# Decoder trunk: the causal mask as a matmul on TensorE, with small moves in the order of work around it

## The chip, the cores and the metric

The kernel runs on one core of one Trainium2 chip. The metric is the device time of one execution in microseconds (us); lower is better. All computing engines have their own queue of instructions and meet by semaphores: TensorE (PE in the profile, its weight loads PEld), VectorE (DVE), ScalarE (ACT), GpSimd (POOL) and SyncE (SP), whose queue issues most of the transfers.

## The reference

Two layers over 512 tokens of width 1024. The first is multi-head latent attention and a dense SwiGLU; the second a pooling mixer and a mixture of eight experts, of which each token takes two. What matters here is the attention's score block and the rows handed to the experts:

```python
for i in range(S // Q_BLOCK):                       # Q_BLOCK = 128
    q0, q1 = i * Q_BLOCK, (i + 1) * Q_BLOCK
    s = (jnp.einsum('bqhd,bkhd->bhqk', q_nope[:, q0:q1], k_nope[:, :q1])
         + jnp.einsum('bqhr,bkr->bhqk', q_rope[:, q0:q1], k_rope[:, :q1]))
    mask = jnp.arange(q0, q1)[:, None] >= jnp.arange(q1)[None, :]
    s = jnp.where(mask, s.astype(jnp.float32), -jnp.inf)
    p = jax.nn.softmax(s, axis=-1).astype(v.dtype)
    outs.append(jnp.einsum('bhqk,bkhd->bqhd', p, v[:, :q1]))
...
xb = xf[buf_tok].reshape(n_blocks, MOE_BLOCK, D)    # rows sorted by expert
yb = lax.map(expert_block, (xb, block_e)).reshape(P, D)
```

## The kernel before

Almost every product is made in three float32r matmuls (`mm3`, L1229 to L1231): each operand is split into a rounded part ("hi", made by ScalarE) and a remainder ("lo", made by VectorE), and lo x hi, hi x lo and hi x hi are summed in PSUM. So each unit of weights, 128 x 1024, is loaded by SyncE's queue, cast by ScalarE (`split`, L823) and subtracted by VectorE (`split`, L1850) before TensorE may use it. Every engine has its order of work written out by hand, and a list on one engine must match the lists on the others.

**Start.** GpSimd makes the identity `ident` (L652, L653), and TensorE fills the time until the first rows of x are there with matmuls nobody reads (`keep_clock`, L1289). Then come the normalised rows, turned by eight transposes (`norm_T`, L1241), and the down projection in four blocks of 128 tokens.

**Latents and rope.** For each block VectorE scales the latents and turns the shared rope key (`latents`), makes the remainders of the turned latents (`latents_lo`, L1909 to L1912), and turns the rope part of the queries (`rotate_q`: three products, then the add at L1888). Some of the remainders stand between the products and the add (`between`). `rope_turned` counts the turned blocks; TensorE starts the first query head when three are there.

**Attention.** Eight heads in four pairs. For each head TensorE makes scores for four blocks of queries, with 128, 256, 384 and 512 keys: one `mm3`, and two matmuls for the rope part (L1391, L1392), each block in a PSUM bank of its own. It then does filler work (projections of the next pair, or in the last pair the first parts of the output projection), turns the probabilities (ten transposes, L1402), does more filler, and multiplies by the values (L1411). Meanwhile VectorE adds the mask `causal` to the last 128 columns of each block in PSUM (L2024), takes the largest of each row (L2025), and after ScalarE's exponential (L942) divides (L2032, L2034). The order is largest 0, largest 1, divide 0, largest 2, divide 1, largest 3, divide 2, divide 3. The fourth block of scores waits for VectorE's remainder of the head before (`o_lo`, L2052). Weight splits lie at four places of each pair (`between`): after the first head's softmax, after the second's, before the second head's output, and at the pair's end.

**Dense SwiGLU.** Its first tiles (`first_tiles`) are done half by half of the tokens, because the last block's rows are turned inside them (`norm_T(2 * T - 1, ...)`).

**Experts.** GpSimd writes the rows to the experts' buffer by eight indirect DMAs (L737), each after the one before has landed, and then loads the block of the second job (L742). TensorE forms the first job's block by itself, and turns the loaded block (L1643) when it comes to the second job.

## Time and profile before

| | us |
|---|---|
| median of 3 runs | 1027.97 |
| lowest and highest | 1027.94, 1028.47 |
| the profiled execution | 1027.94 |
| its span, first to last instruction | 1026.40 |
| TensorE busy in the span | 1013.0 |
| VectorE busy | 597.0 |
| ScalarE busy | 451.4 |
| GpSimd busy | 70.5 |

The profile is of one execution, which took 1027.94 us. Busy time counts an engine's instructions, not its waits for semaphores. TensorE's ends are modelled, so in its timeline the distance from one start to the next is the thing to read, not the duration of one. The granted clock was 0.998 over the span.

### The profile page before, as it was taken

To read this page: it belongs to the slowest core of one execution; us is meant where nothing else is said; L and a number is where in the kernel's file an instruction comes from. 1 tells how busy PE (TensorE), PEld (TensorE's weight loads), DVE (VectorE), ACT (ScalarE), POOL (GpSimd) and SP (SyncE) were. 2 spreads that over 40 slices of the span, in tenths; PEclk is the share of its full clock that TensorE was granted. 3 is DMA by queue.
4 is the path that set the end of the run, shared out by engine and by line. 5 is a ranking of instruction groups with operands and counts; after the bars stand their busy time and mean duration, and the time that the engine had idled before them with its cause. 6 is when DMAs were issued, how large, how long until landed. Compare 5 with 4: busy or idle time off the path is not lost.

```text
span 1026.4 us, 15233 instructions
## 1 busy us (share of the span) xinstructions
PE 1013.0 (99%) x5570; PEld 871.8 (85%) x5570; DVE 597.0 (58%) x840; ACT 451.4 (44%) x602; POOL 70.5 (7%) x135
## 2 busy tenths in 40 slices
PE   9999999999999999999999999999999999999997
PEld 8878887798888888888888999999987888888883
DVE  6677777254344444343436760100689889898987
ACT  6445555244142322222124510010667777777764
POOL 2200000000000001010000011000000000000051
PEclk9999999999999999999999999999999999999999
DMA  9021422535463627273614749896999999999996
GB/s 293 2 82 44 137 67 74 152 104 164 138 188 95 203 85 219 93 214 94 207 41 152 269 157 336 266 343 190 336 369 386 362 393 365 388 370 391 368 395 233
DMA packets 150012, 224.99 MB, mean 219 GB/s; under 512 B 16916, under 2 KB 97812, under 8 KB 149968
## 3 DMA queue, kind: packets, MB, share of 16 engines
q1 hardware_dynamic: 138464, 187.98, 54.6%
q0 software_dynamic: 10688, 35.87, 10.0%
q8 instruction: 28, 0.46, 0.2%
q10 hardware_dynamic: 816, 0.54, 0.2%
q14 instruction: 16, 0.13, 0.0%
HBM read 196.40 MB, written 29.02 MB: 220 GB/s over the span
## 4 chain that ended last, share of the span: by engine, by line
PE 89%; DVE 4%; DMA 3%; ACT 1%; issue 1%; SPq 0%; POOLq 0%; ACTq 0%; DVEq 0%
PE bank L1229 23%; PE bank L1231 23%; PE bank L1230 23%; PE bank L1655 8%; PE bank L1679 4%; PE bank L1411 1%; DMA u_raw<-in_moe_w_down 1%; PE bank L1241 1%; DMA h<-in_x 1%; PE bank L1402 1%; DMA u_raw<-in_moe_w_up 1%; PE bank L1631 1%; PE bank L1550 1%; PE bank L1581 1%; PE bank L1755 1%
## 5 line engine op out<-in xcount | busy, mean ns | idle before, releaser
L2333 DVE TENSOR_TENSOR u_lo<-u_raw,u_hi 128x2048 fp32r<-128x2048 f32 (+1 forms) x104 | 209.6, 2047 | 12.9 <-ACT u_hi L1075 12.2
L1075 ACT CAST u_hi<-u_raw 128x2048 fp32r<-128x2048 f32 (+1 forms) x104 | 178.3, 1723 | 63.3 <-DMA u_raw<-in_moe_w_up 41.2
L1229 PE MATMUL bank<-big_hi,w_lo 128*128 128x512 f32 (+1 forms) x368 | 136.5, 371 | 0.0
L1230 PE MATMUL bank<-big_lo,w_hi 128*128 128x512 f32 (+1 forms) x368 | 136.4, 371 | 0.0
L1231 PE MATMUL bank<-big_hi,w_hi 128*128 128x512 f32 (+1 forms) x368 | 136.4, 371 | 0.0
L1850 DVE TENSOR_TENSOR w_lo<-stage_own,w_hi 128x1024 fp32r<-128x1024 f32 (+1 forms) x89 | 103.5, 1207 | 11.8 <-ACT w_hi L823 11.7
L1012 ACT ACTIVATE scratch<-bank 128x512 f32<-128x512 f32 x21 | 12.5, 597 | 216.3 <-PE bank L1231 216.3
L1229 PE MATMUL bank<-u_hi,nx_lo 128*128 128x512 f32 (+1 forms) x288 | 106.5, 370 | 0.0
L1231 PE MATMUL bank<-u_hi,nx_hi 128*128 128x512 f32 (+1 forms) x288 | 104.5, 363 | 0.0
L1230 PE MATMUL bank<-u_lo,nx_hi 128*128 128x512 f32 (+1 forms) x288 | 104.4, 363 | 0.0
L2117 DVE TENSOR_TENSOR scratch<-scratch,bank 128x512 f32<-128x512 f32 x21 | 14.4, 687 | 150.9 <-ACT scratch L1012 150.9
L823 ACT CAST w_hi<-stage_own 128x1024 fp32r<-128x1024 f32 (+1 forms) x89 | 87.2, 1036 | 8.3 <-DMA stage_own<-in_mla_w_uq 5.5
L1655 PE MATMUL bank<-scratch,u_raw 128*128 128x144 f32 x640 | 81.6, 286 | 0.0
L1229 PE MATMUL bank<-w_hi,act_lo_mem 128*128 128x512 f32 (+1 forms) x216 | 81.0, 375 | 0.1
L1231 PE MATMUL bank<-w_hi,act_hi_mem 128*128 128x512 f32 (+1 forms) x216 | 80.7, 374 | 0.0
L1230 PE MATMUL bank<-w_lo,act_hi_mem 128*128 128x512 f32 (+1 forms) x216 | 80.7, 373 | 0.0
L1655 PEld LDWEIGHTS bank<-scratch,u_raw 128*128 128x128 f32 x640 | 79.7, 190 | 0.1
L1229 PEld LDWEIGHTS bank<-big_hi,w_lo 128*128 128x128 f32 x368 | 69.3, 188 | 12.0 <-DVE big_lo L1870 0.2
L1231 PEld LDWEIGHTS bank<-big_hi,w_hi 128*128 128x128 f32 x368 | 69.3, 188 | 12.0
L1230 PEld LDWEIGHTS bank<-big_lo,w_hi 128*128 128x128 f32 x368 | 69.3, 188 | 11.8
L1229 PEld LDWEIGHTS bank<-u_hi,nx_lo 128*128 128x128 f32 x288 | 54.1, 188 | 9.2 <-issue 1.8
L2339 DVE TENSOR_TENSOR qr_now<-krT,bank 128x144 f32<-128x144 f32 x20 | 6.1, 304 | 95.7 <-ACT krT L1083 95.2
(343 smaller groups left out, 1735.4 us busy)
## 6 DMA issues: line engine op xcount, KB each, us to landing
u_raw<-in_moe_w_gate SPq DMA_DIRECT2D x68, 512.0 KB, 9.1
u_raw<-in_moe_w_up SPq DMA_DIRECT2D x68, 512.0 KB, 10.8
u_raw<-in_moe_w_down SPq DMA_DIRECT2D x64, 512.0 KB, 8.2
stage_own<-in_ffn_w_gate SPq DMA_DIRECT2D x21, 512.0 KB, 5.4
stage_own<-in_ffn_w_up SPq DMA_DIRECT2D x21, 512.0 KB, 9.2
stage_own<-in_ffn_w_down SPq DMA_DIRECT2D x21, 512.0 KB, 4.8
xbuf<-scratch POOLq DMA_DIRECT2D x21, 496.0 KB, 6.0
u_raw<-in_moe_w_down SPq DMA_DIRECT2D x8, 1024.0 KB, 8.6
```

The lines of the kernel that those rows point to most:

```text
L823: s.copy(w_hi[0:parts, sl, 0:n], stage(st)[0:parts, 0:n]).then_inc(weight_hi, 1)
L1012: s.activation(f_silu[:, j % 2, :], bank[2 * (j % 2)][:, :], ACT.Silu).then_inc(silu_ready, 1)
L1075: s.copy(u_hi[u % HIS][0:rows, 0:size], u_raw[u % RAWS][0:rows, 0:size]).then_inc(n_hi, 1)
L1229: t_.matmul(dst, st_lo, mv_hi, start=start, stop=False, skip_group_check=check)
L1230: t_.matmul(dst, st_hi, mv_lo, start=False, stop=False, skip_group_check=check)
L1231: return t_.matmul(dst, st_hi, mv_hi, start=False, stop=stop, skip_group_check=check)
L1241: last = t_.transpose(bank[banks[k // 4]][:, k % 4 * P:k % 4 * P + P], src[:, k * P:(k + 1) * P], ident[:, :])
L1655: last = t_.matmul(dst[:, 0:C], u_raw[u % RAWS][:, at:at + P], xT[:, k, :], start=k == 0, stop=k == KD - 1)
L1679: last = t_.matmul(bank[4 + k // 3][:, col:col + C], u_raw[u % RAWS][0:parts, at:at + P], e_act[0:parts, f % 2, :], start=f == 0 and k % 3 ...
L1850: v.tensor_tensor(w_lo[0:parts, sl, 0:n], stage(st)[0:parts, 0:n], w_hi[0:parts, sl, 0:n], ALU.subtract).then_inc(weight_lo, 1)
L2117: v.tensor_tensor(f_act[:, j % 2, :], f_silu[:, j % 2, :], bank[2 * (j % 2) + 1][:, :], ALU.mult).then_inc(prod_ready, 1)
L2333: v.tensor_tensor(u_lo[u % RAWS][0:rows, 0:size], u_raw[u % RAWS][0:rows, 0:size], u_hi[u % HIS][0:rows, 0:size], ALU.subtract).then_inc(n ...
```

## The change

The mask becomes bfloat16, and a bfloat16 identity `ident_b` is made beside `ident`, before TensorE is let go. Each block of scores gets a sixth matmul, `ident_b` by `causal` into its last 128 columns, which adds the mask in PSUM; VectorE's add is gone. GpSimd no longer waits between the eight scatters. ScalarE's copy of the very first pair's second rope query moves one block later. The splits of the output weights are spread differently over the last two pairs, on both engines. TensorE waits for the third dense unit before the transposes, and not behind them. And VectorE's interleavings of remainders between product and add are taken out: the remainder now comes behind the whole.

```diff
@@ -182,7 +182,8 @@
         cos_t = sb("cos_t", [P, T, ROPE])
         sin_t = sb("sin_t", [P, T, ROPE])
         ident = sb("ident", [P, P])
-        causal = sb("causal", [P, P])
+        ident_b = sb("ident_b", [P, P], BF16)
+        causal = sb("causal", [P, P], BF16)
         ones_b = sb("ones_b", [P, P], BF16)
         before_b = sb("before_b", [P, P], BF16)
         zeros = sb("zeros", [P, P])
@@ -649,9 +650,12 @@
             g = nc.gpsimd
 
             g.memset(eps_t[:, :], EPS).then_inc(eps_ready, 1)
-            link(g.memset(ident[:, :], 0.0))
-            g.affine_select(out=ident[:, :], in_=ident[:, :], compare_op=ALU.not_equal, fill=1.0, base=0,
-                            pattern=[[-1, P]], channel_multiplier=1).then_inc(consts_ready, 1)
+            g.memset(ident[:, :], 0.0)
+            link(g.memset(ident_b[:, :], 0.0))
+            for m in (ident, ident_b):
+                last = g.affine_select(out=m[:, :], in_=m[:, :], compare_op=ALU.not_equal, fill=1.0, base=0,
+                                       pattern=[[-1, P]], channel_multiplier=1)
+            last.then_inc(consts_ready, 1)
             g.memset(causal[:, :], 0.0)
             g.memset(zeros[:, :], 0.0)
             g.memset(ones_b[:, :], 1.0)
@@ -732,8 +736,6 @@
             pool.wait_ge(placed, 1)
             pool.wait_ge(zero_stored, 16 * (FI * FG + YPIECES + E - 1))
             for c in range(2 * T):
-                if c:
-                    pool.wait_ge(scattered, 16 * c)
                 pool.indirect_dma_start(out=xbuf, out_offset=bass.IndirectOffsetOnAxis(ap=dest[:, c:c + 1], axis=0),
                                         in_=xn[:, c % T, :], in_offset=None).then_inc(scattered, 16)
             pool.wait_ge(scattered, 16 * 2 * T)
@@ -933,7 +935,7 @@
             def attention(pair, more, between):
                 def exps(hd):
                     for qb in range(T):
-                        if pair == 0 and hd == 0 and qb == T - 2:
+                        if pair == 0 and hd == 0 and qb == T - 1:
                             q2_out(0, 1)
                         n = (qb + 1) * P
                         at = qb * (qb + 1) // 2 * P
@@ -983,9 +985,9 @@
 
             for pair in range(H // 2 - 2):
                 attention(pair, True, next_pair(pair))
-            attention(H // 2 - 2, True, lambda place: [split("wo", k) for k in ((0,), (1,), (2, 3), (4,))[place]])
+            attention(H // 2 - 2, True, lambda place: [split("wo", k) for k in ((0,), (1, 2), (3,), (4, 5))[place]])
             act.wait_ge(k_done, H)
-            attention(H // 2 - 1, False, lambda place: [split("wo", k) for k in ((5,), (6, 7), (), ())[place]])
+            attention(H // 2 - 1, False, lambda place: [split("wo", k) for k in ((6,), (7,), (), ())[place]])
 
 
             def ffn_split(j):
@@ -1388,8 +1390,9 @@
                         dst, n = bank[qb], (qb + 1) * P
                         mm3(dst[:, 0:n], qn_hi[:, hd, tok(qb)], qn_lo[:, hd, tok(qb)], kn_hi[:, hd, 0:n], kn_lo[:, hd, 0:n],
                             True, False)
-                        t_.matmul(dst[:, 0:n], q2[:, hd, tok(qb)], kr_lo[:, 0:n], start=False, stop=False)
-                        t_.matmul(dst[:, 0:n], q2[:, hd, tok(qb)], kr_hi[:, 0:n], start=False, stop=True
+                        for kr in (kr_lo, kr_hi):
+                            t_.matmul(dst[:, 0:n], q2[:, hd, tok(qb)], kr[:, 0:n], start=False, stop=False)
+                        t_.matmul(dst[:, tok(qb)], ident_b[:, :], causal[:, :], start=False, stop=True
                                   ).then_inc(scores_done, 1)
 
                 def turn(hd):
@@ -1490,9 +1493,9 @@
                     pe.wait_ge(xnT_lo, 2 * T if half else 2 * T - 1)
                     for j in range(2):
                         for q in range(2):
+                            sl = weights("ffn", 2 * j + q)
                             if half == 0 and j == 1 and q == 0:
                                 norm_T(2 * T - 1, T - 1, banks=(4, 5))
-                            sl = weights("ffn", 2 * j + q)
                             for k in range(KD):
                                 last = mm3(bank[2 * j + q][:, at], w_hi[:, sl, k * P:(k + 1) * P], w_lo[:, sl, k * P:(k + 1) * P],
                                            hnT_hi[:, k, at], hnT_lo[:, k, at], k == 0 and half == 0, k == KD - 1 and half == 1,
@@ -1881,13 +1884,12 @@
                 link(v.tensor_tensor(tmp[..., 32:64], q[..., 0:32], sin_t[:, t, 32:64].unsqueeze(2).broadcast_to(half),
                                      ALU.mult))
 
-            def rotate(out_, tmp, q, heads, t, between=lambda: None):
+            def rotate(out_, tmp, q, heads, t):
 
                 product(out_, tmp, q, heads, t)
-                between()
                 return v.tensor_tensor(out_, out_, tmp, ALU.add)
 
-            def latents(t, between=lambda: None):
+            def latents(t):
 
                 dve.wait_ge(c_std, t + 1)
                 v.reciprocal(rms[:, 16 + t:17 + t], rms[:, 16 + t:17 + t])
@@ -1897,7 +1899,6 @@
                 v.scalar_tensor_tensor(c[:, 0:QR], bank[b][:, :], rms[:, 16 + t:17 + t], gain_c[:, 0:QR], ALU.mult, ALU.mult)
                 v.scalar_tensor_tensor(c[:, QR:QR + KVR], bank[b + 1][:, 0:KVR], rms[:, 20 + t:21 + t], gain_c[:, QR:],
                                        ALU.mult, ALU.mult)
-                between()
                 kr = c[:, QR + KVR:DOWN]
                 link(rotate(kr.unsqueeze(1).unsqueeze(1), krope_tmp[:, 0, :].unsqueeze(1).unsqueeze(1),
                             bank[b + 1][:, KVR:KVR + ROPE].unsqueeze(1).unsqueeze(1), 1, slice(t, t + 1)))
@@ -1953,7 +1954,8 @@
             v.reciprocal(band0[:, :, :], band0[:, :, :]).then_inc(counts_inv, 1)
             dve.wait_ge(trig_done, 1)
             dve.wait_ge(gainc_landed, 32)
-            latents(0, lambda: norm_lo(2, 2))
+            latents(0)
+            norm_lo(2, 2)
             norm_lo(3, 3)
             latents_lo(0)
             latents(1)
@@ -1962,13 +1964,13 @@
             for name, n in (("rope", 0), ("rope", 1), ("pair", 0)):
                 split(name, n)
 
-            def rotate_q(t, between=lambda: None):
+            def rotate_q(t):
                 dve.wait_ge(rope_done, t + 1)
                 if t >= 2:
                     dve.wait_ge(rope_ready, t - 1)
                 shape = "p (t h n) -> p t h n"
                 q, out_, tmp = (m.rearrange(shape, t=1, h=H) for m in (bank[rope_bank[t]][:, :], turned[t % 2], rope_tmp))
-                rotate(out_, tmp, q, H, slice(t, t + 1), between).then_inc(rope_turned, 1)
+                rotate(out_, tmp, q, H, slice(t, t + 1)).then_inc(rope_turned, 1)
 
             def rotate_lo(t):
 
@@ -1992,10 +1994,12 @@
                                          bank[6 + b][:, :].rearrange("p (t h n) -> p t h n", t=2, h=2)[:, :, hd, :])
                 last.then_inc(v_ready, 1)
 
-            rotate_q(0, lambda: latents_lo(2))
+            rotate_q(0)
+            latents_lo(2)
             latents(3)
             split("pair", 1)
-            rotate_q(1, lambda: latents_lo(3))
+            rotate_q(1)
+            latents_lo(3)
             rotate_lo(0)
             rotate_q(2)
             rotate_lo(1)
@@ -2020,8 +2024,6 @@
                     def largest(qb):
                         col = 4 * hd + qb
                         dve.wait_ge(scores_done, pair * 8 + col + 1)
-                        own = bank[qb][:, qb * P:(qb + 1) * P]
-                        link(v.tensor_tensor(own, own, causal[:, :], ALU.add))
                         v.tensor_reduce(neg_max[:, col:col + 1], bank[qb][:, 0:(qb + 1) * P], AX.X, ALU.max, negate=True
                                         ).then_inc(max_ready, 1)
 
@@ -2081,8 +2083,8 @@
 
             for pair in range(H // 2 - 2):
                 attention(pair, True, next_pair(pair))
-            attention(H // 2 - 2, True, lambda place: [split("wo", k) for k in ((0,), (1,), (2, 3), (4,))[place]])
-            attention(H // 2 - 1, False, lambda place: [split("wo", k) for k in ((5,), (6, 7), (), ())[place]])
+            attention(H // 2 - 2, True, lambda place: [split("wo", k) for k in ((0,), (1, 2), (3,), (4, 5))[place]])
+            attention(H // 2 - 1, False, lambda place: [split("wo", k) for k in ((6,), (7,), (), ())[place]])
 
 
             def add_attention(t):
```

## Rows read from the trace of the kernel before

**Rows 1.** The page, part 1: busy us (share) xinstructions of TensorE.

```profile
PE 1013.0 (99%) x5570; PEld 871.8 (85%) x5570; DVE 597.0 (58%) x840; ACT 451.4 (44%) x602; POOL 70.5 (7%) x135
```

**Rows 2.** The chain that ended last, in order: start us, us, what.

```profile
87.34 1.09 PE bank L1402 x10
...
99.80 1.09 PE bank L1402 x10
...
663.31 1.01 PE bank L1643 x16
```

**Rows 3.** Timeline, TensorE, last pair's scores: start us, us, what [idle <-releaser].

```profile
154.84 0.28 PE L1391 MATMUL bank<-kr_lo,q 128*128 128x128 f32 x1
154.96 0.28 PE L1392 MATMUL bank<-kr_hi,q 128*128 128x128 f32 x1
...
156.25 0.33 PE L1391 MATMUL bank<-kr_lo,q 128*128 128x384 f32 x1
156.42 0.34 PE L1392 MATMUL bank<-kr_hi,q 128*128 128x384 f32 x1
157.23 0.50 PE L1229 MATMUL bank<-kn_hi,qn_lo 128*128 128x512 f32 x1 [0.48 <-DVE big_lo L2052]
```

**Rows 4.** The same timeline, the turning of that head's probabilities.

```profile
162.56 0.49 PE L1402 MATMUL bank<-ident,scratch 128*128 128x128 f32 x3
...
164.35 0.66 PE L1402 MATMUL bank<-ident,scratch 128*128 128x128 f32 x4 [0.46 <-DVE scratch L2034]
164.77 0.47 PE L1229 MATMUL bank<-w_hi,big_lo 128*128 128x512 f32 x1
```

**Rows 5.** Groups of weight loads by form: busy us, mean ns.

```profile
L1392 PEld LDWEIGHTS bank<-kr_hi,q 128*128 128x128 f32 x32 | 6.1, 190 | 0.4
...
L1613 PEld LDWEIGHTS bank<-picked,before_b 128*128 128x128 bf16 x4 | 0.4, 95 | 0.0
```

**Rows 6.** Timeline, TensorE: first of 14 bfloat16 matmuls, and what follows them.

```profile
595.26 0.17 PE L1613 MATMUL bank<-picked,before_b 128*128 128x8 bf16 x1
...
595.61 0.36 PE L1289 MATMUL bank<-ident 128*128 128x128 f32 x1
```

**Rows 7.** The tile causal: count, ns min/median/max, first and last start.

```profile
L2024 DVE TENSOR_TENSOR bank<-bank,causal x32: 289/292/294, 81.4 to 174.0; 128x128 f32<-128x128 f32 x32
```

**Rows 8.** Timeline of VectorE, last pair's first head.

```profile
157.76 1.22 DVE L1850 TENSOR_TENSOR w_lo<-stage_own,w_hi 128x1024 fp32r<-128x1024 f32 x1
158.89 0.29 DVE L2024 TENSOR_TENSOR bank<-bank,causal 128x128 f32<-128x128 f32 x1
...
163.81 0.48 DVE L2034 TENSOR_SCALAR scratch<-scratch,row_inv 128x512 f32<-128x512 f32 x1
```

**Rows 9.** Timeline of VectorE, the rope stage.

```profile
58.28 0.69 DVE L1909 TENSOR_TENSOR act_lo_mem<-bank,act_hi_mem 128x512 fp32r<-128x512 f32 x1 [0.25 <-ACT act_hi_mem L866]
...
59.42 0.68 DVE L1888 TENSOR_TENSOR scratch<-scratch 128x512 f32<-128x512 f32 x1
```

**Rows 10.** Timeline of TensorE, first query head after the rope stage.

```profile
69.31 0.50 PE L1229 MATMUL bank<-act_hi_mem,w_lo 128*128 128x512 f32 x1 [0.37 <-DVE scratch L1888]
```

**Rows 11.** Timeline of TensorE, the transposes inside the first dense tiles.

```profile
221.93 1.03 PE L1241 MATMUL bank<-ident,scratch 128*128 128x128 f32 x8
```

**Rows 12.** Timeline of VectorE, the remainders of dense units 2 and 3.

```profile
221.29 2.35 DVE L1850 TENSOR_TENSOR w_lo<-stage_own,w_hi 128x1024 fp32r<-128x1024 f32 x2
```

**Rows 13.** Timeline of TensorE, the start of the kernel.

```profile
1.85 5.92 PE L1289 MATMUL bank<-ident 128*128 128x128 f32 x26 [1.85 <-POOL ident L653]
...
18.85 1.09 PE L1241 MATMUL bank<-ident,scratch 128*128 128x128 f32 x8 [0.25 <-DVE scratch L1862]
```

**Rows 14.** Timeline of GpSimd, the selection that makes ident.

```profile
1.51 0.28 POOL L653 TENSOR_SCALAR_AFFINE_SELECT ident<-ident 128x128 f32<-128x128 f32 x1 [0.25 <-POOL ident L652]
```

**Rows 15.** Timeline of GpSimd, first of eight scatters, and the load behind.

```profile
603.58 1.05 POOL L737 DMA_INDIRECT xbuf<-scratch,dest  x1 [37.71 <-DVE dest L2260]
...
646.37 0.80 POOL L742 DMA_DIRECT2D scratch<-xbuf  x1 [4.44 <-DMA xbuf<-scratch,dest]
```

## The prediction

> **What bounds the kernel now.** I read the page first, then the chain that ended last, then timelines around every changed place. On the page TensorE is busy 99% of the span and VectorE, ScalarE and GpSimd far less [rows 1]: the reader is to see that a microsecond of new TensorE work is a microsecond of kernel, unless TensorE was standing still there, and that a microsecond taken off another engine is worth nothing unless TensorE was waiting for it. The chain shows how tight the attention is: the turning of one head's probabilities starts 12.46 us after that of the head before (99.80 less 87.34), the same step for six heads, all of it TensorE [rows 2]. So in the first three pairs the softmax is fully covered by the filler matmuls, and relief on VectorE gives nothing. In the last pair's first head it is not: TensorE waits before the fourth block of scores and again while it turns the probabilities [rows 3, 4]. Those waits are what the change can give back.
>
> **The masks on TensorE.** The change adds one matmul to each of four score blocks of eight heads, 32 in all, 128 columns, bfloat16, with a bfloat16 identity as weights. No row shows this form, so I bound it. Below: a block of 384 columns goes at 0.17 us (156.25 to 156.42) [rows 3], which is 0.057 for 128 columns if only the streaming counts; the 14 bfloat16 matmuls of 8 columns go at 0.025 apiece (595.26 to 595.61) [rows 6], which is the least any could take. Above: 128 columns in the scores go at 0.12 (154.84 to 154.96) [rows 3]. The load of weights decides between them. A bfloat16 load lasts 95 ns against 190 for the float32r one [rows 5], so the identity's own load is hidden. But behind each mask stands another float32r load, and it has only the mask's short stream to hide in; that is the situation in which 128-column matmuls go at 0.11 to 0.12 instead of 0.057. I take 0.11 for each mask: 3.5 us. One thing comes off: the 128-column matmul ahead of the first mask of each head has a quick load behind it now, and may go at 0.057 to 0.07 instead of 0.12, about 0.05 for each of 8 heads, 0.4. Net **+3.1 us**, 0.39 a head; bounds 1.4 (all at the streaming pace, 8 x (4 x 0.057 - 0.05)) and 4.2 (0.13 each).
>
> The Trainium skill, TensorE: Matmul & The Clock Gate, section "Back-to-back issue gap", gives about 81 ns as the sustained spacing at 128 columns where load and matmul alternate. By that the masks would cost 2.6 us instead of 3.5, and the total below would be lower by 0.9 us. No run here shows the figure; the nearest row is the 0.12 above.
>
> **What VectorE loses, and what of it counts.** It loses 32 adds of 0.29 us [rows 7]. In seven heads nothing waits for them. In the last pair's first head TensorE should have started the fourth block at 156.59 (156.42 and 0.17) and started at 157.23, released by VectorE's remainder of the head before: 0.64 lost [rows 3]. The turning took 162.56 to 164.77, 2.21 us, where ten transposes without a wait take 1.09 [rows 2, 4]: 1.12 lost. That makes 1.76 us that could come back. Moving one output-weight split a place earlier takes one 1.13 us piece (157.76 to 158.89) out of VectorE's queue ahead of that remainder [rows 8], so the 0.64 goes. But the same move puts a further split behind it (unit 5 now follows unit 4), so the queue between the end of the previous softmax's tail and this softmax holds as many splits as before: the softmax starts at 158.89 plus the 0.4 by which that head's masks push TensorE. From there to the last division it took 158.89 to 164.29 [rows 8], 5.40 us; four adds fewer are 1.2 less, of which I count 1.0, because some of the exponentials then become what VectorE waits for. Last probabilities at 158.89 + 0.4 + 4.4 = 163.7, four transposes more: 164.2 instead of 164.77, with two heads' masks (0.78) already inside. Given back: 0.57 + 0.78, **-1.4 us**. If this cover fails, the price is that 1.4. The second head of the pair has its splits made shorter, and TensorE did not wait there. The third piece of that list, the query copy moved one block later in the very first head, feeds a matmul that comes a filler later; nothing.
>
> **The rope stage.** Before and after, VectorE's list holds the same pieces; what changes is whether a remainder stands between product and add. In block 0 it waited 0.25 us for ScalarE there, and only then (59.42) came the add of about 0.6 [rows 9]. Put first, the add fills that wait. The other interleaving, in block 1, had no such wait, so it is only an exchange: the turned block is earlier and the remainder 0.3 later. The first query head started at 69.31, held by exactly this chain for 0.37 [rows 10], so what VectorE gains shows: **-0.2 us**, between -0.37 and +0.3 (the remainder that is now late holds the rope matmuls). The same exchange around 31 us costs about 0.1 and is swallowed before the rope stage, which starts from a landed weight.
>
> **The dense tiles.** The wait for unit 2's weights now stands ahead of the eight transposes. They ran from 221.93 [rows 11]; the remainders of units 2 and 3 are one stretch of 2.35 from 221.29 [rows 12], so unit 2's is done after one piece of about 1.22, at 222.51, and seen some 0.06 later. TensorE stands from 221.93 to 222.57, and everything behind it in its queue with it: **+0.64 us** (between 0.5 and 0.7). Before, these transposes covered that time.
>
> **The start.** GpSimd makes a second identity before it lets TensorE begin: a memset and a selection, each at most the 0.28 of the existing selection, about 0.45 [rows 14]. TensorE's first 26 records begin at 1.85 and end at 7.77 [rows 13]; the transposes behind them come that much later. The next gate, at 18.85, was itself waited for by 0.25 [rows 13], so most is hidden: **+0.1 us**, bounds 0 and +0.9 (see the rivals).
>
> **The scatters.** Without the waits the eight go out back to back from 603.58. The block behind them is asked for at 646.37 [rows 15] and used by TensorE only at 663.31 [rows 2]: 16.9 us of room. GpSimd was not on the path: **0**. If that cover were gone, the price would be whatever TensorE then waits for the block.
>
> **Sum.** The profiled execution took 1027.94 us with a span of 1026.40; the median of the three runs is 1027.97, the same. +3.1 - 1.4 - 0.2 + 0.64 + 0.1 = +2.2, so **1030.2 us**. Behind the dense tiles I expect the same work in the same time, only later, since weight loads there are released by TensorE's own progress.
>
> **The rivals.** 0.2% is about 2 us, and about what a measurement of this kernel can tell from no change; slower by over 0.2% begins at 1030.03.
> - *Masks at the streaming pace.* The float32r load behind a mask is pulled ahead and hidden, so a mask costs 0.057: masks +1.4 and, with smaller shifts, 1.3 given back. Total +0.7, 1028.7 us: not slower. For it: the bfloat16 loads are half as long [rows 5] and go at 0.025 [rows 6]. Against it: 128-column float32r matmuls never went under 0.11. It decides as soon as a mask costs less than about 0.10. Chance 0.18.
> - *In between.* Masks at about 0.08, total +1.4, 1029.3: 0.07. The skill's spacing, named above, is that case.
> - *Nothing given back.* The softmax of the last pair ends late all the same, because VectorE does one more split ahead of it: +3.6, 1031.6. Against it: the count of pieces is unchanged. 0.08.
> - *The start at the slow pace.* The first 26 records go at 0.23 apiece (5.92 by 26) [rows 13]; if TensorE, started later, still goes so in the eight transposes behind them, they take 1.8 instead of 0.9, and the kernel +0.9 more, 1031.0. 0.05.
> - *Scatters crowd the weights.* Eight blocks written at once share the DMA engines with expert weights; if those fell behind TensorE, a stall of up to 3 us, 1033. TensorE's lead over its loads speaks against it. 0.04.
> - *The masks are hidden and the early scatters help*, faster by over 0.2%: I see no wait of 2 us left to fill. 0.03.
>
> **How the numbers follow.** The forecast has 0.55, with a range of its own from 1029.6 to 1031.2; some 0.38 of it lies above 1030.03 and 0.17 below. Slower: 0.38 + 0.08 + 0.05 + 0.04 = 0.55. Same: 0.17 + 0.18 + 0.07 = 0.42. Faster: 0.03. The range for 8 in 10 takes in the streaming case at the low end and the case without give-back at the high end: 1028.6 to 1031.6.
>
> **What would show it.** In the changed profile: from one head's turning to the next 12.85 us instead of 12.46 in the first six heads; next to each mask a step of about 0.11 to the following matmul; the fourth block of the last pair's first head without a wait, and about 0.4 us of waiting left in the turning there; the first query head near 69.1; the transposes of the dense tiles released by VectorE after a wait near 0.6; the load behind the scatters some 20 us earlier with nothing else moved. The prediction is wrong if the step behind a mask is near 0.06, or if the distance from the dense tiles to the end is not the one of before.

## The result, and the profile after

The changed kernel took **1037.47 us** (median of 4 runs, 1036.23 to 1038.67), the kernel before 1028.03 beside it: ratio 1.0091, 95% interval 1.0074 to 1.0108. That is 9.4 us slower where 2.2 us were forecast, and outside the range. The profiled execution took 1036.58 us, with a span of 1034.6 against 1026.4, so its trace has 8.2 us to explain.

The page's line for the engines (busy us, share of the span, instructions), for [rows 1]:

```profile
PE 1018.2 (98%) x5602; PEld 874.7 (85%) x5602; DVE 588.7 (57%) x808; ACT 449.8 (43%) x602; POOL 69.6 (7%) x137
```

The chain that ended last (start us, us, what), for [rows 2] and for the job behind it:

```profile
87.78 1.09 PE bank L1405 x10
...
100.68 0.33 PE bank L1405 x3
...
183.17 2.16 PE bank L1414 x8
...
607.03 6.12 PE bank L1658 x50
613.15 0.14 issue
...
616.54 1.04 issue
617.59 2.32 PE bank L1658 x9
619.91 2.31 PE bank L1682 x16
```

Four rows of the chain of before that answer to these:

```profile
181.07 2.16 PE bank L1411 x8
...
604.51 7.84 PE bank L1655 x64
612.35 1.96 PE bank L1679 x16
614.31 3.92 PE bank L1655 x32
```

Read them from the top. The turnings are 12.90 us apart (100.68 less 87.78) instead of 12.46. The last head's values come 2.10 us later (183.17 less 181.07), the first expert's columns 2.52 later (607.03 less 604.51): up to here the forecast of +2.2 is nearly met. Then comes what it did not have. The first 64 matmul records of the expert take 12.88 us (607.03 to 619.91) instead of 7.84, and the next 16 take 2.31 instead of 1.96: +5.4 in one place. Of these, 3.8 us are standing: the first 55 records fill 10.56 us (607.03 to 617.59) where 55 take 6.74 at 0.1225 each. The other 1.6 are a slower pace behind it: nine records in 2.32 instead of 1.10, then the sixteen. The remaining +0.3 collects behind it.

What happened there, in the timeline of all engines (start us, us, engine, line; in brackets the idle time before and its releaser):

```profile
606.10 1.05 POOL L739 DMA_INDIRECT xbuf<-scratch,dest  x1 [37.46 <-DVE dest L2262]
...
609.26 1.28 ACT L1085 ACT_TABLE_LOAD   x1 [1.80 <-issue]
...
614.73 0.41 PE L1658 MATMUL bank<-scratch,u_raw 128*128 128x144 f32 x2 [1.03 <-issue]
615.07 0.96 POOL L739 DMA_INDIRECT xbuf<-scratch,dest  x1 [0.31 <-issue]
616.17 0.38 PE L1658 MATMUL bank<-scratch,u_raw 128*128 128x144 f32 x1 [1.03 <-issue]
617.59 2.32 PE L1658 MATMUL bank<-scratch,u_raw 128*128 128x144 f32 x9 [1.04 <-issue]
617.69 0.29 ACT L1085 ACTIVATE krT<-bank 128x144 f32<-128x144 f32 x1 [7.15 <-remote]
```

and in the windows of 2 us (busy time and count of each engine, then the granted clock, the DMA share and GB/s):

```profile
612.00:614.00 2.00, 1.56 (x12) 1.35 (x11) 1.42 (x8) 0.00 (x0) 1.39 (x3) 1.00 0.93 365
614.00:616.00 2.00, 0.41 (x2) 0.19 (x1) 0.00 (x0) 0.00 (x0) 1.69 (x2) 1.00 0.99 385
616.00:618.00 2.00, 0.79 (x3) 0.78 (x4) 0.00 (x0) 0.29 (x1) 0.03 (x1) 0.77 0.98 383
618.00:620.00 2.00, 2.00 (x10) 2.00 (x10) 0.30 (x1) 0.06 (x1) 0.00 (x0) 0.50 0.46 184
620.00:622.00 2.00, 2.00 (x16) 2.00 (x16) 0.30 (x1) 0.23 (x1) 0.80 (x1) 0.88 0.22 15
```

GpSimd issues the eight scatters one per 1.27 us from 606.10 to 616.03. The signs of trouble come in this order. ScalarE's activation waits for TensorE's count of finished columns, which TensorE had earned by about 611 (32 records at 0.1225 us from 607.03); it starts at 617.69, and the profile can't place its releaser ("remote"). TensorE runs on for some 20 records after that count, in the middle of a row of matmuls that wait for nothing, and stops at 613.3, with its gaps put down to issue. It gets one or two matmuls at a time, and runs again at 617.59, 1.56 us after the last scatter's end. So it waited for no data: no weight and no block of tokens was late. Then its clock is granted at half (0.50, that is 1.2 GHz) for 3.4 us from 617.1, after a stretch in which it had done little.

### The profile page after: what moved, and what is told of

Its sections match the earlier page's. It is cut to its first block, busy times and chain, and to the rows that moved or that the text cites. A ratio compares the mean times of both kernels' runs of the same rounds, so it can differ in the third digit from the quotient of the medians.

```text
span 1034.6 us, 15267 instructions
## 1 busy us (share of the span) xinstructions
PE 1018.2 (98%) x5602; PEld 874.7 (85%) x5602; DVE 588.7 (57%) x808; ACT 449.8 (43%) x602; POOL 69.6 (7%) x137
## 4 chain that ended last, share of the span: by engine, by line
PE 87%; DVE 6%; DMA 3%; issue 2%; ACT 2%; POOL 0%; POOLq 0%; SPq 0%; DVEq 0%; ACTq 0%
PE bank L1231 22%; PE bank L1233 22%; PE bank L1232 21%; PE bank L1658 8%; PE bank L1682 4%; PE bank L1414 1%; DMA scratch<-ybuf,from_y 1%; PE bank L1243 1%; DVE w_lo L1853 1%; PE bank L1394 1%; PE bank L1405 1%; DMA ybuf<-n_y 1%; PE bank L1634 1%; PE bank L1553 1%; PE bank L1584 1%
```

## The experiments

Eighteen kernels beside the changed one. "Over before" is the ratio to the kernel before as it ran on the same chip in the same hour (its medians there 1028.9 to 1029.4). The question of the first four: which part of the change costs the 9 us?

**The waits put back** (the changed kernel, with the kernel before's waits):

```
+                if c:
+                    pool.wait_ge(scattered, 16 * c)
                 pool.indirect_dma_start(...)
```

> The changed kernel with the waits between the eight scatters put back, nothing else. Its trace shows TensorE 2.5 us late where the first expert job begins, and 7.6 us late at that job's first down projection (619.91 against 612.35), with the engines standing still from about 613.4 to 617.6 while the scatters fill the DMA engines. Theory A (the burst of scatters starves the engines): that stop goes, and the time is about 1030.4, from 1029.9 to 1030.9. Rival B (the stop comes from the masks or from the shift of the work before it, and the scatters only stand beside it): the time stays at 1036 to 1038.

Measured: 1031.77 us, ratio 1.0028 (1.0018 to 1.0038), span 1029.2. The stop is gone; all 64 records of the first expert's columns in one piece of the chain:

```profile
607.11 7.84 PE bank L1660 x64
```

**The waits taken out of the kernel before, and nothing else:**

> The kernel before with the waits between the scatters taken out, nothing else. Theory A: the stop of about 5 us at the first expert job is there without any mask, so 1033.0 to 1036.0 us. Rival B: 1028, as before. If part of the loss comes back later, behind weight loads that run ahead while TensorE stands, it is nearer to the lower end.

Measured: 1034.65 us, 1.0052 (1.0037 to 1.0067), span 1031.4. The stop is there: 53 records, four gaps, and the 16 records behind the columns at 616.86 instead of 612.35 (chain of this kernel):

```profile
604.38 6.63 PE bank L1653 x53
614.79 2.08 PE bank L1653 x8
616.86 2.48 PE bank L1677 x16
```

Together the two show it. The missing waits cost 5.4 us on the kernel before (1.0052). On the changed kernel they cost 6.5 us by the ratios (1.0091 less 1.0028) and 5.7 between the medians, which are of different hours. All the rest costs 2.6 to 2.9 us.

**The masks alone** (the kernel before, with the second identity and the masks on TensorE, VectorE's adds gone):

> The kernel before with the masks as matmuls and VectorE's add gone, and the second identity, nothing else (the splits of the output weights, the rope stage, the dense tiles and the scatters as before). A head should take 12.9 us instead of 12.46 from turning to turning, 0.44 more, as the changed kernel's chain shows; 8 heads are 3.5 us. Of the 1.76 us that TensorE waited in the last pair, I expect about 1.0 back, since the split is not moved. Forecast 1030.5, from 1030.0 to 1031.0. If the masks were cheap (0.06), 1028.9; if the whole slowing were theirs, 1036.

Measured: 1030.72 us, 1.0015 (1.0005 to 1.0024), span 1028.4. Dense transposes at 224.00, first expert columns at 606.32, 1.81 us later than before.

**A quarter of the bytes.** Each scatter writes only a quarter of each row, to other addresses; the experts then read rows that are not there, so the output is not the reference's:

```
-  out=xbuf, ... in_=xn[:, c % T, :]
+  out=xbuf.rearrange("r (q n) -> (r q) n", q=4), ... in_=xn[:, c % T, 0:D // 4]
```

> The changed kernel with the burst kept, but each scatter writes only the first quarter of each row (256 of 1024 values, to other addresses), so the experts' rows are not the right ones and a quarter of the bytes are moved; the number of scatters, of rows and of GpSimd instructions is the same. Theory A by bytes (the DMA engines are full of the scatters' data): the time in which they are full shrinks from about 11 us to 3 or 4, the stop goes or falls under 1 us, and the time is about 1030.4 to 1031.5. Rival C (GpSimd's issuing back to back, 0.96 us each, is what holds the others): the stop stays near 5 us and the time near 1036.

Measured: 1036.17 us, 1.0064 (1.0046 to 1.0082). The DMA engines are at 0.18 to 0.37 in the stop, and it is nearly as long (3.5 us of standing instead of 3.8):

```profile
614.00:616.00 2.00, 0.57 (x2) 0.32 (x2) 0.00 (x0) 0.00 (x0) 1.69 (x2) 1.00 0.37 131
```

My first theory, that 4 MB at once crowd something out of the DMA queues, fell with this. The next four asked whether it is GpSimd's issuing.

**The burst in mid-loop** (one line ahead of the scatters, `pool.wait_ge(expert_used, AHEAD + 12)`):

> The changed kernel with one line more: GpSimd waits, ahead of the eight scatters, until TensorE has used twelve more columns of the first expert, so that the burst (about 10 us) falls near 628 us, when every engine has been through its loop over that expert's tiles, instead of at 606, when each enters the loop for the first time. Theory A (eight indirect scatters issued back to back by GpSimd hold up the issue of instructions on every engine, whenever they come): TensorE stands still for 4 to 5 us in mid-loop too, with waits put down to issue, the granted clock falls behind it, and the time stays 8 to 9 us over the kernel before. Theory C (only an engine that comes to code it has not run yet is held up, since it is that code which does not arrive): no stop in the loop, the time is that with the waits put back, 2.5 to 3.5 us over the kernel before. If the first fetch of code of the next block (after 24 more matmuls) is what fails, a shorter stop, in between.

Measured: 1032.58 us, 1.0034 (1.0020 to 1.0048), span 1030.4. The stop is there in code that had run before, but short (1.4 us of standing), and ScalarE shows the same sign, an activation 4.5 us late (timeline):

```profile
643.03 2.98 PE L1659 MATMUL bank<-scratch,u_raw 128*128 128x144 f32 x23 [0.78 <-issue]
...
643.11 0.29 ACT L1086 ACTIVATE krT<-bank 128x144 f32<-128x144 f32 x1 [10.06 <-remote]
```

So neither theory was right in its price: new code is not needed for the stop, and its length is not fixed.

**Pairs, and fours** (a wait for all landings ahead of each second scatter; ahead of the fifth):

> The changed kernel, with GpSimd waiting for all scatters to land before each second one: two are issued back to back, then a landing. Theory A1 (what counts is how long GpSimd issues without a break: the stop began 7 us after the first of the eight in all three kernels with the burst): a pair takes 2.3 us of issuing, no stop, the time is 2.5 to 3.5 us over the kernel before. Theory A2 (any scatter issued while another is under way costs the other engines a stop): four short stops of about 0.5 to 1 us of TensorE, 4 to 6 us over the kernel before.

> The changed kernel, with GpSimd waiting for all scatters to land once, before the fifth: four are issued back to back, then four more. With eight, TensorE ran out of instructions 7.2 us after the first scatter's start (9.4 us in mid-loop) and got the next ones 1.4 us after the last scatter's end, in all four kernels with the burst. Theory A1 (an engine has several us of instructions in hand, gets no more while GpSimd issues scatters without a break, and only a burst longer than that stops it): four take 4.8 us of issuing, so TensorE does not stop, and the time is 2 to 3.5 us over the kernel before, like the pairs. Theory A4 (it is the number of bytes or scatters under way, and three or more already stop it): a stop of 1 to 3 us, 4 to 6 us over the kernel before.

Measured: 1031.12 us, 1.0020 (1.0011 to 1.0030), and 1031.73, 1.0023 (1.0012 to 1.0034). TensorE has no stop in either. But with the fours ScalarE's first activation is 1.1 us late, where pairs have it at 611.04 (timeline of the fours):

```profile
612.28 0.29 ACT L1087 ACTIVATE krT<-bank 128x144 f32<-128x144 f32 x1 [1.52 <-PE bank L1660]
```

**Paced, nobody waits for a landing** (six linked memsets of an unused tile between two scatters, which then start 2.8 us apart):

> The changed kernel, with six small memsets of an unused tile, each waited for by GpSimd itself, between one scatter and the next: no scatter waits for a landing, but they start some 3.5 to 4 us apart, as they did before with the waits, instead of 1.27 us apart. Theory A1 (the density of issuing counts): no stop, 2.5 to 3.5 us over the kernel before. Theory B (that up to two scatters overlap in the DMA queues counts, or the missing wait as such): a stop, 5 to 9 us over it.

Measured: 1032.35 us, 1.0033 (1.0021 to 1.0046), span 1029.1. No stop.

**Plain transfers, 8 and then 32** (`pool.dma_start(xbuf[c * P:(c + 1) * P, :], xn[:, c % T, :])`, and the same in four quarters each; the experts read other rows, so the output is not the reference's):

> The changed kernel, with each of the eight indirect scatters replaced by a plain transfer of the same 512 KB from the same tile to rows in their own order, issued by GpSimd back to back: the experts then read other rows than the router chose, so the output is not the reference's. Theory A3 (the indirect form counts: GpSimd reads 128 addresses and writes a descriptor for each): no stop, 2.5 to 3.5 us over the kernel before. Rival (4 MB in the DMA queues at once, or any burst from GpSimd's queue, does it): a stop of 3 to 5 us, 6 to 9 us over it. A quarter of the bytes left the stop, so I expect A3.

> The changed kernel, with the eight scatters replaced by 32 plain transfers issued by GpSimd back to back, four quarters of each row block, to rows in their own order (the experts then read other rows than the router chose, so the output is not the reference's). The eight plain transfers took only 4.2 us of issuing, which is less than the 7.2 us that TensorE had in hand, so they did not tell the indirect form from the time that issuing takes; 32 take about 17 us. Theory A3 (it is the indirect form, for which GpSimd reads addresses and writes descriptors one by one): no stop, 2.5 to 4 us over the kernel before. Theory A5 (any issuing by GpSimd without a break for over 7 us does it): TensorE stops some 7 us after the first transfer for 5 to 10 us, 10 to 16 us over it.

Measured: 1032.66 us, 1.0034 (1.0023 to 1.0046), and 1032.19, 1.0026 (1.0013 to 1.0038). No stop in either, though the 32 kept GpSimd issuing for 17.07 us without a break:

```profile
606.33 17.07 POOL L741 DMA_DIRECT2D xbuf<-scratch  x32 [37.46 <-DVE dest L2263]
```

Issuing as such is not it, then. Two more varied the length of the burst.

> The changed kernel, with GpSimd waiting once for all scatters to land, before the seventh: six are issued back to back, then two. Theory A1 (no engine gets new instructions while GpSimd issues scatters without a break, until about 1.4 us after the last one's end; TensorE had 7.2 us in hand here): the sixth ends 7.4 us after the first one's start, so new instructions come at 8.8 us, and TensorE stops once, for 1 to 1.7 us; the time is 3.5 to 5 us over the kernel before. Rival (a stop needs all eight, by their bytes in the queues): no stop, 2 to 3 us over it, as with four and four.

> The changed kernel with sixteen scatters in the burst instead of eight: each is followed by the same scatter into a second buffer that nobody reads. Theory A1: TensorE stops 7 us after the first scatter as before, gets a matmul or two at a time while the burst lasts, and runs again 1.4 us after the sixteenth one's end, some 10 us later than in the changed kernel; the time is 17 to 21 us over the kernel before. Rival (the stop has a length of its own, a piece of code that comes late once): the stop stays at 4 to 5 us, 8 to 10 us over it.

Measured: six and two 1031.82 us, 1.0029 (1.0016 to 1.0042); sixteen 1031.14, 1.0022 (1.0010 to 1.0034). **No stop in either.** Sixteen should have stopped TensorE for 14 us; TensorE has no gap, and the activation is on time (timeline of that kernel):

```profile
611.15 0.29 ACT L1087 ACTIVATE krT<-bank 128x144 f32<-128x144 f32 x1 [0.45 <-PE bank L1660]
```

That threw out the theory that the length of the burst sets the stop. (One execution of each, not the one in the trace, took 1035.22 and 1034.89 us; whether TensorE stopped in those is not known. The same holds for 1034.70 us with the met wait below.) Stranger still, the kernel with six has the same scatters at the same spacing up to the sixth (612.63), and yet its activation is on time at 611.09, where the changed kernel's was already late. The last two kernels varied the row of instructions (`if c == 4: pool.wait_ge(placed, 1)`, a wait long met) and the addresses (each second scatter into another buffer, so half the rows are missing and the output is not the reference's).

> The changed kernel with one line more: between the fourth and the fifth scatter GpSimd waits for a semaphore that has long been there, so that nothing is waited for and the eight scatters keep their 1.27 us from one to the next. Sixteen scatters without a break and six without a break did not stop TensorE, eight did in four kernels, so the length of the burst is not the cause (theory A1 has fallen). Theory D (what counts is GpSimd's sequencer, which runs ahead over eight scatters in a row and then stands at its wait; an instruction between them breaks the row): no stop, ScalarE's first activation at 611 us, 2 to 3.5 us over the kernel before. Theory E (it is the eight scatters by their times and addresses, whatever stands between them): the stop is there, 8 to 10 us over it.

> The changed kernel, where the second, fourth, sixth and eighth scatter go to a second buffer of the same size that nobody reads, so half of the routed rows are missing and the output is not the reference's: the first eight of the kernel with sixteen scatters went to two buffers in turn as well. Theory F (it is the addresses: a run of scatters into one buffer does it, two in turn don't): no stop, 2 to 3.5 us over the kernel before. Theory D (eight in a row and then a wait, wherever they go): the stop is there, 8 to 10 us over it.

Measured: 1032.39 us, 1.0032 (1.0022 to 1.0043), and 1031.51, 1.0027 (1.0016 to 1.0037). No stop in either. In the first the scatters keep their 1.27 us, and only an instruction that waits for nothing stands among them:

```profile
611.49 0.96 POOL L741 DMA_INDIRECT xbuf<-scratch,dest  x1 [0.30 <-issue]
...
611.20 0.29 ACT L1087 ACTIVATE krT<-bank 128x144 f32<-128x144 f32 x1 [0.44 <-PE bank L1660]
```

So eight scatters at these times and addresses do not suffice (theory E). By the second kernel, neither do eight in an unbroken row, wherever they go (theory D).

**The smaller terms.** The dense tiles' order put back, on top of the waits:

```
-                            sl = weights("ffn", 2 * j + q)
                             if half == 0 and j == 1 and q == 0:
                                 norm_T(2 * T - 1, T - 1, banks=(4, 5))
+                            sl = weights("ffn", 2 * j + q)
```

> The changed kernel with the waits between the scatters put back and the dense tiles' transposes again behind the wait for the weights, as in the kernel before. In the traces so far the step costs 0.64 us (the transposes start at 224.64 us with it and at 224.00 in the kernel with the masks alone, from turnings at the same time). If that is its price: the first expert column starts 0.6 to 0.7 us earlier than with the waits put back alone (606.4 instead of 607.1), and the time is 1.8 to 2.6 us over the kernel before. If the masks' give-back or the earlier split is what differs between the two, it starts at 607.1 as well.

Measured: 1031.19 us, 1.0016 (1.0006 to 1.0026). The transposes start at 224.13 against 224.72 with the waits back alone, the expert's columns at 606.28 against 606.94: the step costs 0.6 to 0.7.

**The splits alone**, in the kernel before:

> The kernel before with one part of the change: the splits of the attention's output weights on ScalarE and VectorE in their new places (k = 2 with 1, 4 and 5 behind, 7 alone). Theory: the wait of TensorE ahead of the fourth block of the last pair's first scores (0.48 us, for big_lo) goes, as it is gone in the changed kernel, but the turning's waits (1.12 us, for the divided probabilities, behind VectorE's mask adds) grow by as much, since VectorE has the same work: within 0.3 us of the kernel before. Rival: both shrink and the time is 0.5 to 1.2 us below it.

Measured: 1030.21 us, 1.0006 (0.9996 to 1.0015). By itself it moves the dense transposes from 221.93 to 222.59, 0.66 us later. The run times do not tell it from nothing; the trace says it is no gain.

**The mask on TensorE for one head of eight**, the first of the last pair, with the splits moved and then with them in their old places:

```
+  here = pair == H // 2 - 1 and hd == 0
   last = t_.matmul(dst[:, 0:n], q2[:, hd, tok(qb)], kr_hi[:, 0:n], start=False, stop=not here)
+  if here:
+      last = t_.matmul(dst[:, tok(qb)], ident_b[:, :], causal[:, :], start=False, stop=True)
```

> The kernel before, with the splits moved as in the changed kernel and the causal mask added on TensorE for one head of eight, the first of the last pair, where TensorE waited for VectorE (0.48 us ahead of the fourth block, 1.12 us in the turning); the other seven heads keep VectorE's adds. Theory: the four mask matmuls cost 0.43 us, both waits go but for 0.25 us, so the turning and all behind it come 0.8 to 1.0 us earlier, and the time is 0.6 to 1.0 us under the kernel before. Rival: the second head of the pair, whose adds are back on VectorE, waits for it in turn and takes the gain: within 0.3 us of the kernel before.

> The kernel before with the causal mask on TensorE for the first head of the last pair alone, and the splits of the attention's output weights where they were. With the splits moved this kernel was 0.8 us under the kernel before (0.999, 0.9981 to 0.9999), and the splits alone made the first expert column 0.65 us later. If the splits cost their own 0.65 us here too: the first expert column starts 0.5 us earlier than with them (603.3), and the time is 1.0 to 1.6 us under the kernel before. If the mask's gain swallows them, as in the kernel with all masks (224.13 against 224.00 us at the dense tiles): within 0.3 us of it, 0.5 to 1.1 us under the kernel before.

Measured: 1028.57 us, 0.9990 (0.9981 to 0.9999), span 1026.0; and 1028.77, 0.9991 (0.9982 to 1.0000), span 1025.7. In the second the turning has no wait left and the head's values come 0.92 us earlier than before (166.86 against 167.78, chain):

```profile
166.86 2.16 PE bank L1418 x8
```

The trace gains 1.2 us at the first expert (603.13 against 604.35); the run times show 0.9 us by the ratio and only 0.3 between the medians, at the edge of what they can tell. These two are the only versions ahead of the kernel before, by 0.1%.

## Why the prediction was wrong

**The step that failed: the scatters, at 0.** The step looked for who waits for the scattered block, found 16.9 us of room, and was right in that: nothing waited for it, and its load was asked for at 620.64. Where the stop did not come, scatters without waits cost nothing that the medians show: six and two, a met wait and sixteen stand at 1.0029, 1.0032 and 1.0022 over before, with the waits 1.0028. But in the changed kernel TensorE stopped, which cost 5.4 us in its trace (3.8 of standing and 1.6 of the slower pace behind it) and 5.5 to 5.7 us in medians (1034.65 less 1029.17 with the burst alone; 1037.47 less 1031.77 with the waits back). The step asked what a wait protects on its own queue and not what else the burst could disturb. The rival "Scatters crowd the weights" had the right place and a stop of up to 3 us, but named late weights; none was late, and a quarter of the bytes changed nothing. Its chance was 0.04.

**What causes the stop is not settled.** Shown, by one trace of each kernel: it is there in four kernels, and in all four GpSimd's program has exactly eight indirect scatters to one buffer with no other instruction among them. It is not there with six and two, with four and four, in pairs, with a wait among them that is already met, with sixteen or eight that go to two buffers in turn, with memsets among them, nor with plain transfers. Bytes, share of the DMA engines, time of issuing, length of the burst and first use of code are each excluded by a run. A wait among them and a second buffer each removed it alone. Not shown: whether the row and the addresses are the cause, or something that goes with them, such as where instructions lie in memory.

**What the traces show of the step between.** A packed trace also holds the times at which each semaphore was raised, which no view above prints. TensorE raises the count that ScalarE waits for after each 16 records. With the waits back this happens at 609.08, 611.04, 613.00 and 614.96 us. In the changed kernel it happens at 609.68, 617.67, 617.83 and 619.92, though its first 32 records were made by 610.95 and 48 by 612.9. So the second count was 6.7 us late and the third 4.9, and ScalarE started 0.02 us after the second. The other three kernels with the stop show the same (the late count is at 614.86 with the burst alone, 617.57 with the quarter rows, 643.08 in mid-loop). That the count was late, and late before TensorE stopped, is therefore shown. That TensorE stops because counts are pending is only argued.

Each of the eight scatters raises the landing semaphore 16 times, 128 in all. The traces of the kernels that wait for each landing, and of those with pairs, six and two, two buffers, sixteen, a met wait and plain transfers, have every one. Those with the stop have 54, 53, 36 and 82 of 128. Two without a stop lack some as well: four and four has 93, with ScalarE 1.1 us late, and the one with memsets has 84. So the disturbance is wider than "eight in an unbroken row"; only the stop of TensorE is bound to that here. Late code is not in sight: the one transfer of instructions in the changed kernel from 600 to 620 us, 16 KB from 607.13, took 1.1 us, and the kernel with the met wait has the same one.

One rival stands untested. Every execution measured here comes with a recorded span and clock, and records are missing just where the stop is. Whether TensorE would stop if nothing was recorded, no run shows.

**The masks: mechanism right, 0.04 a head too small.** The step from turning to turning is 12.90 instead of the forecast 12.85, so 0.43 a head instead of 0.39, and 3.5 us for eight heads instead of 3.1. The cost fits the reason the text gave, the float32r load behind the mask, but shows one matmul later than expected (timeline, TensorE):

```profile
159.22 0.34 PE L1394 MATMUL bank<-kr_hi,q 128*128 128x384 f32 x1
159.40 0.23 PE L1395 MATMUL bank<-causal,ident_b 128*128 128x128 bf16 x1
159.44 0.47 PE L1231 MATMUL bank<-kn_hi,qn_lo 128*128 128x512 f32 x1
159.75 0.39 PE L1232 MATMUL bank<-kn_lo,qn_hi 128*128 128x512 f32 x1
```

The mask's successor starts 0.04 us after it, and the one after that 0.31 later, where 512 columns take 0.23 further on. A mask and its shadow are 0.35 less 0.23, 0.12 us; the mean of a head's four is 0.11. The text named a step behind the mask near 0.06 as a sign that it was wrong. The step is 0.04, and the mask was dear all the same, so that sign looked one matmul too early. The 0.05 that it took off for the matmul ahead of the first mask did not come there either (0.12 us up to the mask, 0.11 before). The spacing that the text cited from the Trainium skill, TensorE: Matmul & The Clock Gate, section "Back-to-back issue gap", would have made 2.6 us of 32 masks, an estimate; the trace does not agree, with its 3.5.

**The give-back: right in size, not in what brings it.** The fourth block starts without a wait (159.44 above), as forecast, and the turning has one of 0.25 us left where 0.4 was expected [rows 4]:

```profile
165.99 0.66 PE L1405 MATMUL bank<-ident,scratch 128*128 128x128 f32 x4 [0.25 <-DVE scratch L2036]
```

Eight heads of masks are 3.5 us, the values of the last head are 2.10 later: 1.4 came back, as forecast. The text had the moved split clear the 0.64 ahead of the fourth block, but the split was not needed for it. With the masks alone, the splits in their old places, the values of the last head start at 183.18 instead of 183.17: the same give-back. Alone, the splits only made the dense tiles 0.66 later, for the wait ahead of the fourth block went and the turning's waits grew by more. With the masks alone the fourth block still waited, but for 0.21 us instead of 0.48.

**The start and the rope stage** came to +0.1 together at the first query head, where -0.1 was forecast. TensorE starts at 2.24 instead of 1.85; the first query head comes at 69.42 instead of 69.31, with its wait gone [rows 10]. By the first turning nothing of it is left: 87.78 less 87.34 is the 0.44 of one head's masks.

**The dense tiles: right.** The wait is VectorE's remainder, as forecast:

```profile
224.64 1.09 PE L1243 MATMUL bank<-ident,scratch 128*128 128x128 f32 x8 [0.48 <-DVE w_lo L1853]
```

0.6 to 0.7 us by the kernel with the order put back; 0.64 was forecast.

**Behind the dense tiles** the same work took the same time up to the scatters: 382.22 us from the transposes to the expert's columns, 382.42 before. The text named the distance from the dense tiles to the end as one thing that would prove it wrong, and it did: the rest of it, from the expert's columns on, grew by 5.7 us.

So the forecast holds for the change without its burst: 1.0028 over before is 2.9 us (2.6 between the medians), and the sum said 2.2. The terms' own errors are 0.4 (masks) and 0.1 to 0.2 (start and rope).

## What to carry to other kernels

Taking out a wait is not free because nobody needed the data: it changes what runs at the same time, and the price can fall on an engine that has nothing to do with it. Judge such an edit by itself, look for idle time put down to "issue" on the engine that sets the end, and put the cheap break back if it is there; here even a wait already met was enough. Work moved from a covered engine to the one that sets the end costs its full time; move it only in the one place where that engine was waiting.

## What the runs showed of the hardware that was not expected

- In the four kernels with eight indirect scatters in a row to one buffer, TensorE stood for 3.5 to 3.8 us (1.4 in mid-loop) with no data to wait for, and a count that it had earned reached ScalarE 4.5 to 6.7 us late, at a DMA share of 0.99 and equally at 0.37. 32 plain transfers in a row, over 17 us, did neither.
- A matmul of 128 columns in bfloat16 among float32r ones costs 0.11 us on average, about twice its stream of 0.057, and the delay shows in the second matmul behind it.
- The clock can fall without TensorE standing. Five of the 20 traces, the changed kernel's and that with the waits back among them, have a second stretch at half clock where the wide expert jobs end, while TensorE is busy all through (windows of the changed kernel):

```profile
744.00:746.00 2.00, 2.00 (x12) 1.71 (x11) 1.11 (x1) 0.55 (x1) 0.00 (x0) 0.50 1.03 390
```

  Sixteen records took 3.29 us there instead of 1.78. Much of it came back later: in the kernel before TensorE waited for weights in the narrow jobs (8.09 us of a load stood on its chain at 765.57), and waits less when it comes later.
